# Two transformer blocks on one core: gate slabs inside the state-space scan, z at the head of its stage, key evictions split between two engines, causal taps started earlier and kept on one engine, the gating norm ahead of the last taps

## The reference, cut to what matters

```python
# first block
u = rms_norm(x, norm_mix_g) @ w_in            # 672 mla, 1544 fox, 2576 ssm, 3 x 1024 gates
y_a = mla_branch(u_mla, ...) @ w_br_mla       # 8 heads; q and k normed per head, rope, softmax
y_b = fox_branch(u_fox, ...) @ w_br_fox       # 8 heads; decay bias from log_sigmoid(f_raw + b_f)
y_c = ssm_branch(u_ssm, ...) @ w_br_ssm
g = sigmoid(u_gate + b_gate)                  # 3 x 1024
x = x + (g[0] * y_a + g[1] * y_b + g[2] * y_c) @ w_out
x = x + conv_ffn(rms_norm(x, norm_ffn_g), ffn_w_up, ffn_conv_w, ffn_conv_b, ffn_w_down)

def ssm_branch(u):
    z, xBC, dt_raw = split(u)                               # 1024, 1536, 16
    xs, Bm, Cm = split(silu(causal_dwconv(xBC, conv_w, conv_b)))   # width 4
    dt = softplus(dt_raw + dt_bias)
    y = ssd_scan(xs, dt, -exp(A_log), Bm, Cm) + xs * D      # 16 heads of 64, state 128
    return rms_norm(y * silu(z), norm_g)

# second block: four branches from one norm, each gated
y_a = spatial_gating(gelu(sg_u), gelu(sg_v), ...)   # layer norm of v, then a 128 x 128 mix
y_b = gated_linear_attention(...)
y_c = band_chunk_attention(...)
y_d = silu(layer_norm(causal_dwconv31(c_a * sigmoid(c_g)) + dw_b))   # 512 channels, width 31
h = h + sum_n(sigmoid(xn @ w_gate[n] + b_gate[n]) * (y_n @ w_branch[n])) @ w_out
h = h + relu(rms_norm(h) @ w_ff1)**2 @ w_ff2
h = h + sigmoid(rms_norm(h) @ w_ple_gate + b_ple_gate) * (p @ w_ple);  out = rms_norm(h)
```

## Time and profile before

| | |
|---|---|
| time, three runs | 2300.03, 2308.07, 2327.18 us; median 2308.07 |
| the profiled execution | 2319.43 us, its span 2317.7 us |
| granted TensorE clock, mean | 0.964 of full |
| TensorE busy | 2175.5 us, 94% |
| DVE, ACT, POOL busy | 1133.9, 814.7, 132.3 us |

### The profile page before, as it was taken

How to read it: one execution, slowest core, us unless ns; L and a number is a source line. 1 busy time by engine, 2 the same in 40 slices (tenths; PEclk the granted TensorE clock), 3 DMA queues, 4 the chain that set the end, 5 groups by cost and what they waited for, 6 DMA issues and landing times.

```text
span 2317.7 us, 24798 instructions
## 1 busy us (share of the span) xinstructions
PE 2175.5 (94%) x10133; PEld 1794.5 (77%) x10133; DVE 1133.9 (49%) x1649; ACT 814.7 (35%) x1154; POOL 132.3 (6%) x115
## 2 busy tenths in 40 slices
PE   5989988998999999999999998979999999999996
PEld 5877876977888778888777776768888878888875
DVE  3734455374343456536535878452344444334235
ACT  4455642423232243313332352543233243123232
POOL 0000000010000000000003950000000000000000
PEclk9998899988999999999999999989999999999998
DMA  3221012200322333233233202212232223223221
GB/s 117 82 73 37 1 37 66 90 1 19 109 92 91 127 91 91 92 106 94 73 96 122 91 20 70 85 37 91 91 107 94 91 79 103 91 92 108 92 100 55
DMA packets 166495, 185.58 MB, mean 80 GB/s; under 512 B 4711, under 2 KB 129894, under 8 KB 166382
## 3 DMA queue, kind: packets, MB, share of 16 engines
q1 hardware_dynamic: 162568, 174.96, 23.8%
q10 hardware_dynamic: 3110, 6.90, 0.8%
q0 software_dynamic: 704, 2.13, 0.3%
HBM read 181.86 MB, written 2.12 MB: 79 GB/s over the span
## 4 chain that ended last, share of the span: by engine, by line
PE 87%; DVE 6%; ACT 4%; issue 1%; DMA 1%; ACTq 0%; POOL 0%; DVEq 0%; POOLq 0%
PE ps L334 25%; PE ps L335 25%; PE ps L336 25%; PE ps L426 3%; PE ps L446 2%; PE ps L329 2%; PE ps L437 1%; ACT arena L1097 1%; DVE WL L1535 1%; PE ps L409 1%; PE ps L614 1%; PE ps L642 1%; PE ps L460 1%; ACT WH L1068 0%; DVE X L2007 0%
## 5 line engine op out<-in xcount | busy, mean ns | idle before, releaser
L1535 DVE TENSOR_TENSOR WL<-W,WH 128x2048 fp32r<-128x2048 f32 (+2 forms) x168 | 378.6, 2259 | 490.0 <-ACT WH L1068 468.2
L334 PE MATMUL ps<-HH,WH 128*128 128x512 f32 x1416 | 556.3, 393 | 11.1 <-DVE HL L1558 6.4
L335 PE MATMUL ps<-HL,WH 128*128 128x512 f32 x1416 | 553.3, 391 | 0.0
L336 PE MATMUL ps<-HH,WL 128*128 128x512 f32 x1416 | 553.2, 391 | 0.0
L1068 ACT ACTIVATE WH<-W 128x2048 fp32r<-128x2048 f32 (+2 forms) x168 | 314.2, 1876 | 319.9 <-DMA W<-in_w_ff_dram 109.6
L334 PEld LDWEIGHTS ps<-HH,WH 128*128 128x128 f32 x1416 | 267.3, 189 | 70.5 <-DVE WL L1535 7.8
L336 PEld LDWEIGHTS ps<-HH,WL 128*128 128x128 f32 x1416 | 267.2, 189 | 55.8
L335 PEld LDWEIGHTS ps<-HL,WH 128*128 128x128 f32 x1416 | 267.5, 189 | 55.5 <-issue 0.2
L334 PE MATMUL ps<-WH,arena_r 128*128 128x512 f32 (+1 forms) x616 | 240.7, 391 | 9.4 <-DVE WL L1535 6.4
L335 PE MATMUL ps<-WL,arena_r 128*128 128x512 f32 (+1 forms) x616 | 239.8, 389 | 0.0
L336 PE MATMUL ps<-WH,arena_r 128*128 128x512 f32 (+1 forms) x616 | 239.7, 389 | 0.0
(11 more groups left out here) (323 smaller groups left out, 2451.4 us busy)
## 6 DMA issues: line engine op xcount, KB each, us to landing
W<-in_w_in_dram SPq DMA_DIRECT2D x51, 1024.0 KB, 5.2
W<-in_w_ff_dram SPq DMA_DIRECT2D x32, 1024.0 KB, 5.2
W<-in_ffn_w_up_dram SPq DMA_DIRECT2D x44, 512.0 KB, 5.1
W<-in_w_gate_dram SPq DMA_DIRECT2D x16, 1024.0 KB, 4.9
W<-in_ffn_w_down_dram SPq DMA_DIRECT2D x10, 1024.0 KB, 5.0
W<-in_w_out_dram SPq DMA_DIRECT2D x8, 1024.0 KB, 5.0
W<-in_w_branch_dram SPq DMA_DIRECT2D x8, 1024.0 KB, 5.0
W<-in_w_br_ssm_dram SPq DMA_DIRECT2D x4, 1024.0 KB, 4.9
```

Of the source, the lines that this page charges most:

```text
L334: pe.matmul(out_, st[0], mv[0], start=first, stop=False)
L335: pe.matmul(out_, st[0], mv[1], start=False, stop=False)
L336: return pe.matmul(out_, st[1], mv[0], start=False, stop=last)
L1535: dve.tensor_tensor(WL[:, j % RING, 0:n], W[:, j % RING, 0:n], plain(WH[:, j % RING, 0:n]), ALU.subtract).then_inc(slab_lo, 1)
```

## The change

- **The scan.** Two of the 20 slabs of gates1 are multiplied before the scan (PRE_GATES), nine inside it (SCAN_GATES): one after the state update of each chunk, one after its first two mixes, one after the last mix. Nine stay in gates1. The three calls of keep_clock in the scan go. ACT's sigmoids and DVE's sums go with the slabs, and so do their splits. The y rows of mla and fox are split at the head of ssm and in the third chunk; the finished scan rows are kept over `xt`. Buffers move (MG, G of one place instead of two, the input of wout1 at 8192).
- **The ssm stage.** z comes first, in two halves of 512 columns; dtsm is multiplied in fox, after its KT turns; softplus, `ss` and `cdec` follow in and behind z. The accumulators of the filter are a ring of three, and TensorE turns tile j-2 after the product of tile j, where it was j-1.
- **mla and fox.** fsm is multiplied ahead of fq; the KT evictions are made by DVE (`dve_turn`), the QT evictions by ACT as before. The places of the fox slabs in the score steps move up.
- **Taps.** All 124 are on DVE. convin multiplies cg 0, ca 0, cg 1, ca 1 by half, and 16 taps are made in that stage; band has 10 after each split and one in two of three score steps.
- **sgu.** The 128x128 weights are turned and copied ahead of the su slabs; the root and the norm of v stand ahead of the last taps, of which 5 are left. In gla, one more slab is split before the filter's mean and one before its scaling.

```diff
-    FK_AT, FT_AT, FV_AT = 4, 10, 18
-    FQ_NORM, FK_NORM = 7, 13
+    FK_AT, FT_AT, FV_AT = 1, 8, 16
+    FQ_NORM, FK_NORM = 4, 11
...
+    order = first + second + [(2, *x) for x in branch_order(8)]
+    PRE_GATES = order[:2]
+    SCAN_GATES = [[x] for x in order[2:11]]
+    REST_GATES = order[11:]
...
-        DVE_CHANNELS = 3
-        TAPS_SLAB = 6
+        FIRST_TAPS = 8
+        TAP_ORDER = [(j, c) for cs in ((0, 1), (2, 3)) for j in range(FIRST_TAPS) for c in cs]
+        TAP_ORDER += [(j, c) for j in range(FIRST_TAPS, TAPS) for c in range(4)]
+        TAPS_SLAB = 10
...
                 w = slab(KT, P, win(2208, 2208 + P))
                 gemm_f("fsm", w, KT, 0, 1, hn)
                 slab_read()
+                gemm_t_long("fq", full, 672, hnt)
                 pe.wait_ge(heads_ready, 1)
...
+                w = slab(KT, P, win(4776, 4776 + P))
+                gemm_f("dtsm", w, KT, 0, 1, hn)
+                slab_read()
...
+                gemm_t_long("z", full, 2216, hnt, 0)
+                gemm_t_long("z", full, 2728, hnt, 1)
...
                         gemm_f("xbc", w, KT, c * P, 1, hn, j)
-                        if 0 <= j - 1 < 10:
-                            turn_conv(j - 1)
+                        if 0 <= j - 2 < 10:
+                            turn_conv(j - 2)
...
+                for x in PRE_GATES:
+                    gate_slab("G1", *x)
...
-                    keep_clock(b, KEEP["chunk"])
...
-                                keep_clock(b, KEEP["state"])
...
                                       start=True, stop=True).then_inc(pe_done, 1)
+                    for n, kind, cc, j in SCAN_GATES[2 * t]:
+                        gate_slab("G1", n, kind, cc, j)
...
                             b = bank(("yd", t, q // 2))
-                            keep_clock(b, KEEP["mix"])
...
                             arow(3)
+                            for n, kind, cc, j in SCAN_GATES[2 * t + 1]:
+                                gate_slab("G1", n, kind, cc, j)
                             if t > 0:
                                 yturn(t - 1)
+                for n, kind, cc, j in SCAN_GATES[2 * NT]:
+                    gate_slab("G1", n, kind, cc, j)
                 yturn(NT - 1)
...
-            def pool_conv():
...
-                act_turn("mla", "KT", at(19456, HEADS, S), DQ, 1)
...
+            def dve_turn(tag, dst, d, gcol):
+                for h in range(HEADS):
+                    b = use(dve, (tag, "KT", h))
+                    freed(dve.tensor_scalar(dst[0:d, h, :], b[0:d, :], gq[0:d, gcol:gcol + 1], None, ALU.mult),
+                          (tag, "KT", h))
...
-                    if 2 <= c < 12:
-                        take(c - 2)
...
                     mix(1)
+                    for n, kind, cc, j in SCAN_GATES[2 * t]:
+                        gate_sum("G1", n, kind, cc, j)
                     diff(2)
                     diff(3)
-                    if t > 0:
-                        keep(t - 1)
                     mix(2)
                     mix(3)
-                    for half in range(2):
+
+                    def diagonal(half):
                         sl = slice(half * 512, (half + 1) * 512)
                         b = use(dve, ("yd", t, half))
                         freed(dve.tensor_tensor(x[:, sl], x[:, sl], b[:, :], ALU.add), ("yd", t, half))
+                    diagonal(0)
+                    for n, kind, cc, j in SCAN_GATES[2 * t + 1]:
+                        gate_sum("G1", n, kind, cc, j)
+                    if t == 2:
+                        rows_low("G1", 1)
+                    if t > 0:
+                        keep(t - 1)
+                    if t == 0:
+                        taken(dve, ("z", NT - 1, 1))
...
-                    if s >= 4 and s % 2 == 0:
+                    if s >= 4 and s % 3 != 0:
...
                 for i in range(slab_of["su", 0] - 2, slab_of["su", 0]):
                     split(i + 1)
                     taps(12)
-                copied(("sv", NT - 1, 0))
-                split(slab_of["su", 0] + 1)
+                b = use(dve, "swT")
+                freed(dve.tensor_copy(swT, b[:, :].rearrange("p (g i) -> p g i", g=4)), "swT")
+                taken(dve, "swT")
+                dve.memset(swT[64:P, :, 0:64], 0.0).then_inc(sgu_weights_ready, 1)
+                taken(dve, ("sv", NT - 1, 0))
                 for t in range(NT):
                     link(dve.bn_stats(bn[:, t, :], v[:, t, :]))
                     link(dve.bn_aggr(mv[:, t, :], bn[:, t, :]))
                 link(dve.tensor_copy(stat[:, 0:4], mv[:, :, 1]))
-                taps(DVE_CHANNELS * TAPS - tapped[0])
...
                 link(dve.tensor_tensor(v, v, bc(g.unsqueeze(1), [P, NT, 512]), ALU.mult))
                 dve.tensor_tensor(v, v, bc(bb.unsqueeze(1), [P, NT, 512]), ALU.add).then_inc(sgu_values_ready, 1)
-                b = use(dve, "swT")
-                freed(dve.tensor_copy(swT, b[:, :].rearrange("p (g i) -> p g i", g=4)), "swT")
-                taken(dve, "swT")
-                dve.memset(swT[64:P, :, 0:64], 0.0).then_inc(sgu_weights_ready, 1)
+                taps(len(TAP_ORDER) - tapped[0])
                 split(slab_of["su", 3] + 1)
                 dst, tmp = at(0, 4, S), at(14848, S)
...
                     if c == 1:
+                        split(slab_of["cg", 2] + 1)
+                        taps(FIRST_TAPS)
```

More of the change, by code:

```diff
@@ L821, in pe_sgu @@
                 tr.then_inc(pe_done, 1)
+                for j in range(2):
+                    w = slab(KT, 256, win(256 * j, 256 * j + 256, "w_in_2"))
+                    gemm_f("su", w, KT, 0, 2, hn, 2 * j)
+                    slab_read()
                 swT, v = at(12800, 4, P), at(10240, NT, 512)
@@ L1044, in _ @@
                     program[s]()
[L1045 to L1053 removed]
+                boundary(pool, gpsimd_end, k)
         @block.scalar
@@ new lines, in act_ssm, with rows_high @@
+                for n, kind, cc, j in SCAN_GATES[2 * NT]:
+                    gate_out("G1", n, kind, cc, j)
+            GATES = {"G1": ("b_gate", 0, 3), "G2": ("b_gate2", KT, 4)}
+            def rows_high(tag, n):
+                kt = 8 if (tag, n) == ("G1", 2) else 4
+                before = n - 2 if tag == "G2" else 0 if (tag, n) == ("G1", 1) else -1
+                if before >= 0:
+                    result(((tag, "b", before, 1), 3))
+                if (tag, n) == ("G1", 2):
+                    taken(act, ("yT", NT - 1, 1))
+                ys = split_rows(tag, n)[0]
+                for k in range(kt):
+                    act.activation(in_tiles(ys[:, k, :]), whole_row(tag, n, k), ACT.Copy).then_inc(hi_ready, 1)
@@ new lines, in gate_out @@
+            def gate_out(tag, n, kind, cc, j):
+                bname, sums, count = GATES[tag]
+                G, MG, mg, _ = gate_places(tag)
+                ring = G.shape[1]
+                i = 2 * n + cc
+                if kind == "g":
+                    if (tag, n, cc, j) == ("G1", 0, 0, 0):
+                        act.wait_ge(y_split, 4)
+                    for c in (2 * j, 2 * j + 1):
+                        b = result(((tag, "g", n, cc), c))
+                        if i >= ring:
+                            taken(act, ((tag, "b", (i - ring) // 2, (i - ring) % 2), c))
+                        freed(act.activation(G[:, i % ring, c, :], b[:, :], ACT.Sigmoid,
+                                             bias=pcol(bname, n * KT + cc * 4 + c)), ((tag, "g", n, cc), c))
+                    return
+                cs = range(4) if (tag, n) != ("G1", 2) else (2 * j, 2 * j + 1)
+                for c in cs:
+                    split(slab_of[((tag, "b", n, cc), c)] + 1)
+                    if n == count - 1:
+                        k = 4 * cc + c
+                        act.wait_ge(sum_ready, sums + k + 1)
+                        act.activation(mg[:, k, :], MG[:, k, :], ACT.Copy).then_inc(hi_ready, 1)
```

461 lines of the change are left out of this document (230 added, 231 removed).

## The result

The changed kernel took 2231.8 us (median of four runs, 2225.63 to 2233.96) against 2308.8 before: ratio **0.9675** with a 95% interval of 0.9641 to 0.971. That is 77 us less by the medians and 75 by the ratio. On a second chip the same pair gave 0.9679 (0.9649 to 0.9709), with medians of 2232.2 and 2301.3 us, 69 apart. The forecast was 2222, its range 2202 to 2248.

What follows compares the result with a forecast made beforehand. TensorE, busy 94% of the span, was taken as the bound. Gains of 6, 22.4, 47 and 11 us, together 86.4, took 2319.43 to 2233.0; less 11.36 to the median gave 2221.7, range 2202 to 2248.

Steps and rivals of the forecast that it cites:

- rival 2: Scan: the clock falls without the dummies; 24 us more at 0.86 (2246), 72 at 0.67 (2294); chance 0.06.
- the 5 us given back: Scan: allowance for entry, a first chunk without state and jitter, taking the gross 52.1 us gain to 47.
- Rivals 1 and 4: Scan: chain longer than slab, 20 us back, 2242 to 2246, chance 0.11; slabs handed over late, 123 us more, 2345, 0.03.
- Rival 3: Outside the scan: the places give little, half of 39.4 us is lost, 2241; chance 0.06.
- my seven: Scan: seven more table loads on ACT, costing nothing off the path, 9.0 us if all were on it.
- the second 4.65 us of evictions: MLA: with keys on DVE, two sets of 8 evictions run side by side; first scores 6 us sooner.
- The split that I feared: sgu: a split of 2.29 us ahead of the norm, leaving the 9.9 us wait only just gone.
- the offset: Whole kernel: the median lies 11.36 us below the profiled execution, so 2233.0 becomes 2221.7.
- the sum: Whole kernel: gains of 6 (MLA), 22.4 (ssm), 47 (scan) and 11 (sgu), together 86.4 us.
- the other three terms: Gains outside the scan: MLA 6 us, the ssm stage 22.4, sgu 11.

Runs made afterwards that it cites:

- e7: The changed kernel with the key evictions of MLA and FoX back on ScalarE, fsm still ahead of fq: 2223.1 us, ratio 0.9649.
- e6: The changed kernel with each channel tile turned one product after its own, as before, ring of three accumulators kept: 2235.3 us, ratio 0.9705.
- e9: The kernel before, unchanged, run again for a second profile: 2298.2 us.
- e12: The changed kernel with fsm multiplied behind fq again, keys still on VectorE, and the split ahead of them now for fk's slab: 2241.2 us, ratio 0.9733.
- e4: The changed kernel with arow, the rows' spread, as a product over all 128 partitions in place of 16: 2219.3 us, ratio 0.9635.
- e10: The changed kernel with arow over 128 partitions, key evictions on ScalarE, no dummies ahead of FoX's and the band attention's first scores: 2205.8 us, ratio 0.9586.

## Why the prediction held, and which of its steps did not

**The scan, right in what fills it, 4.7 us short.** The chain of a chunk fits behind the slab, as worked out: no wait is left in it, where I had given back 5 us for waits. What came instead is rival 2 in a mild form, the clock, and at a place that I had not named: behind arow, 3.4 us each time, 10.2 us in all. The work at full clock was right: 47.4 us in my sum, 47.0 in the trace. So the term that was mis-sized is the 5 us given back, and for the wrong reason: 47.0 + 10.2 = 57.2, where I had 47.4 + 5 = 52.4. ACT was busy 67.26 us and DVE 98.79 in the scan; I had 55 and 95. Its own terms, 28.91 + 17, make 46 for ACT and not 55; what came on top of the nine splits is 9.0 us of sigmoids, 10.3 of table loads and 2.5 of splitting the rows.

**The other rivals.** Rivals 1 and 4 needed TensorE to wait for WL or the mix in the scan; there is no such wait. Splits run ahead of use. Rival 3 did not come either: the places outside the scan gave 6.3, 24.4 and 12.3 us, 43.0 for 39.4. Loads of tables in the scan went from 8 to 16:

```profile
L1286 ACT ACT_TABLE_LOAD x6 | 7.7, 1283 | 0.1
L1345 ACT ACT_TABLE_LOAD x6 | 7.7, 1283 | 0.1
L1092 ACT ACT_TABLE_LOAD x4 | 5.1, 1283 | 0.1
```

Eight more than before, one more than my seven, each 1283 ns, and TensorE waited for none of them. The drain of some 1380 ns beside each load that the Trainium skill gives (ScalarE: Activation LUTs, What ACT_TABLE_LOAD costs) shows as no idle time here either: it is 0.1 us in all ahead of the loads of each line. The time does not tell, since ScalarE has slack.

**MLA: the right number for a wrong reason.** I counted the second 4.65 us of evictions as the gain, and fsm's move as what makes room for them. e7 shows that fsm's move is enough: the wait of 4.28 us between the turns and the low clock behind it go with it.

**ssm.** 24.4 for 22.4. A turn was charged at 0.65 us. A tile with its turn now takes 5.91 us from turn to turn, 5.46 of it the product by the price that I used, so a turn costs 0.45: over ten, the 2.0 us. e6 confirms the lag as the cause of 14.4 of the 24.4, and that the third accumulator alone does next to nothing (12.1 us of waits against 13.5). The rest is z in wider matmuls and what moved with it, which no run separates.

**sgu.** 12.3 for 11: the wait of 9.9 and 2.2 of low clock. The split that I feared costs 2.29 and is covered, with 4.2 us to spare.

**Taps.** Nothing, as forecast: convin and band are together 171.4 us long before and after. In band alone, 125.3 us both times, VectorE's busy time fell although it has more taps, for GpSimd's 104.30 us are gone:

```profile
1254.40:1379.70 125.30, 124.37 (x628) 96.13 (x629) 100.29 (x185) 52.03 (x119) 104.30 (x61) 1.00 0.19 59
```

```profile
1178.90:1304.20 125.30, 124.38 (x628) 96.12 (x629) 93.45 (x214) 52.46 (x119) 0.00 (x0) 1.00 0.19 60
```

That is what the Trainium skill (GPSIMD Engine Reference, 1. Specifications) would have by its shared interfaces, and the 0.67 against 1.17 of the earlier trace rows had shown.

**The step that failed is the offset.** I took 11.36 us off the sum because the profiled execution of before ran that much above the median, as if it lay outside the terms. It lay in them: e9 shows 11.3 us of low clock in the MLA attention and 4.5 in the scan that a faster execution hasn't. The 86.4 of the sum met 87.0 between the profiles, but between medians it is 77, so 2222 became 2232. Set against e9 in place of the first profile, the scan gives 37.8 us and not 42.3, the attention is 6.9 us longer after the change and not 4.4 shorter, and the whole is 65.8 us. So the -4.4 of the attention in the table, where I had 0 within 3, cannot be told from this spread.

That 86.4 met 87.0 is luck in part: the scan fell 4.7 short, wout1 lost 2.5 (the first wait for WL 2.43 us in place of 1.9, and low clock behind it) and gla 2.3, and 4.4 of the attention, 3.6 of the other three terms and 1.5 of the rest made up for them. Neither wout1 nor gla was tried. One step of the range is off too: 2207 less the 8 of the spread is 2199, not 2202, which changes nothing here.

## What to carry to other kernels

Work that is ready at any time, such as a projection of an early input, belongs in the holes of a serial stage: nine slabs there were worth 45 to 50 us, and dummies in the same holes nothing of the time (2276.7 us without, 2276.0 with). Ask of two edits made together which one moves the releaser: the split evictions looked like the gain and a moved small product was. When a run undoes one of them, see in its trace that nothing else took the place of the old wait, as a split did in e12. When a sum is built on one profile, take a second one first, and treat stretches in which the clock falls as ranges.

## What the runs showed of the hardware

- Six of the eight groups of 16 matmuls with 16 rows of 128 in the scan are followed by 3.4 us at half clock, though TensorE never stops; the same matmuls over all 128 rows are not (clock 0.93 against 1.00 over 155.4 and 142.5 us; e4, and again e10). A group over 16 rows isn't faster either: 2.05 against 1.95 us, and 1.98 against some 1.78 to the start of what follows.
- The same scan code lost 6.8 to 13.7 us to the low clock in five kernels, and was 145 us long without that loss in each.
- The scan without slabs and dummies ran at 0.56 of the clock, 81% busy.
- The same code ran the MLA attention in 102.4 us at clock 0.95 and in 113.7 at 0.85.
- FoX's and the band attention's first scores need no dummies directly behind full-speed products: without them (e10) these stretches were 3.3 and 2.8 us shorter.
